# Token-major projections in chunks of 512 columns, with the first mixer's operand copied into class order

## The reference, cut to what matters

```python
# mixer of block 0 (A: banded attention, B: dilated attention)
qa, ka, va, qb, kb, vb = jnp.split(xn @ w_in, splits, axis=-1)   # va 256, vb 768 columns
# dilated attention gathers by stride: residue classes of the token number
t.reshape(bsz, sub, dil, B_SLOTS, dh).transpose(0, 2, 1, 3, 4)
# mixer of block 1
q, k, v = jnp.split(xn @ w_in, 3, axis=-1)                       # v 1024 columns
# mixer of block 2: of w_in_2, the columns i (512), vs (128), vw (128) and ng (24 gates)
...
```

## Time and profile before

| | us |
|---|---|
| median of 3 runs | 3481.54 |
| lowest and highest run | 3477.34, 3484.66 |
| span of the profiled execution, first to last instruction | 3476.3 |

### The profile page before, as it was taken

The page is one execution under the profiler, slowest core; times in us unless marked ns, Lnnn a source line. Parts: engine busy times, 40 slices in busy tenths (PEclk is TensorE's granted clock), DMA queues, the critical chain, the costliest instruction groups (busy, mean ns, idle before and its releaser), DMA issues.

```text
span 3476.3 us, 49224 instructions
## 1 busy us (share of the span) xinstructions
PE 3343.7 (96%) x16800; PEld 2705.7 (78%) x16800; DVE 1999.1 (58%) x2493; ACT 1753.2 (50%) x2114; POOL 1211.2 (35%) x625
## 2 busy tenths in 40 slices
PE   8999999999999999999999999899889999999996
PEld 6888888678888788888678888688766788787774
DVE  4335672663354433541463333457776699888888
ACT  5552212645533555321545533423563688888883
POOL 3444441044444444444134444342203222222224
PEclk9999999999999999999999999999999999999998
DMA  3225321023244222443422233222002899999997
GB/s 125 96 95 171 112 100 37 2 85 97 97 150 141 85 97 97 151 132 110 128 72 95 96 94 103 76 95 82 31 1 77 333 402 414 408 410 401 393 397 307
DMA packets 128103, 555.40 MB, mean 160 GB/s; under 512 B 19344, under 2 KB 19600, under 8 KB 100112
## 3 DMA queue, kind: packets, MB, share of 16 engines
q1 hardware_dynamic: 112896, 520.59, 41.5%
q0 software_dynamic: 14976, 33.58, 2.6%
q10 hardware_dynamic: 144, 0.08, 0.0%
HBM read 531.62 MB, written 41.94 MB: 165 GB/s over the span
## 4 chain that ended last, share of the span: by engine, by line
PE 60%; issue 25%; POOL 7%; DVE 5%; ACT 2%; DMA 1%; POOLq 0%; DVEq 0%; SPq 0%; ACTq 0%
PE ps L731 17%; PE ps L733 16%; PE ps L732 16%; POOL w_lo L1762 7%; PE ps L1189 2%; PE ps L751 1%; PE ps L892 1%; PE ps L1268 1%; PE ps L917 1%; PE ps L902 1%; PE ps L1018 1%; PE ps L1000 1%; PE ps L979 0%; DMA big<-in_exp_gu 0%; PE ps L1208 0%
## 5 line engine op out<-in xcount | busy, mean ns | idle before, releaser
L1762 POOL TENSOR_TENSOR w_lo<-stage_buf,w_hi 128x1024 fp32r<-128x1024 f32 (+1 forms) x396 | 971.8, 2454 | 1554.9 <-ACT w_hi L1344 1554.9
L1344 ACT ACTIVATE w_hi<-stage_buf 128x1024 fp32r<-128x1024 f32 (+1 forms) x396 | 413.9, 1045 | 1254.9 <-PE ps L733 1204.8
L731 PE MATMUL ps<-x_hi,w_hi 128*128 128x512 f32 x1984 | 776.1, 391 | 8.7 <-POOL w_lo L1762 7.9
L732 PE MATMUL ps<-x_lo,w_hi 128*128 128x512 f32 x1984 | 774.9, 391 | 0.0
L733 PE MATMUL ps<-x_hi,w_lo 128*128 128x512 f32 x1984 | 774.5, 390 | 0.0
L731 PE MATMUL ps<-hid,w_hi 128*128 128x512 f32 x1312 | 519.0, 396 | 2.6 <-issue 1.7
L733 PE MATMUL ps<-hid,w_lo 128*128 128x512 f32 x1312 | 511.7, 390 | 0.0
L732 PE MATMUL ps<-hid,w_hi 128*128 128x512 f32 x1312 | 510.8, 389 | 0.0
L731 PEld LDWEIGHTS ps<-x_hi,w_hi 128*128 128x128 f32 x1984 | 374.2, 189 | 90.7 <-POOL w_lo L1762 9.6
L733 PEld LDWEIGHTS ps<-x_hi,w_lo 128*128 128x128 f32 x1984 | 374.3, 189 | 78.0
L732 PEld LDWEIGHTS ps<-x_lo,w_hi 128*128 128x128 f32 x1984 | 374.2, 189 | 77.5
(11 more groups left out here) (388 smaller groups left out, 5121.8 us busy)
## 6 DMA issues: line engine op xcount, KB each, us to landing
stage_buf<-in_gu SPq DMA_DIRECT2D x176, 512.0 KB, 3.3
big<-in_exp_gu SPq DMA_DIRECT2D x72, 1024.0 KB
h_buf<-in_exp_gu SPq DMA_DIRECT2D x72, 1024.0 KB
s_buf<-in_exp_dn SPq DMA_DIRECT2D x72, 1024.0 KB
slot_rows<-stage_buf SPq DMA_DIRECT2D x72, 512.0 KB
stage_buf<-in_down SPq DMA_DIRECT2D x64, 512.0 KB, 3.6
stage_buf<-in_down SPq DMA_DIRECT2D x32, 384.0 KB, 3.1
sil_buf<-in_ada SPq DMA_DIRECT2D x24, 512.0 KB, 4.1
```

The lines of the kernel that those rows point to most:

```text
L731: nc.tensor.matmul(o, a_hi, b_hi, start=start, stop=False)
L732: nc.tensor.matmul(o, a_hi, b_lo, start=False, stop=False)
L1344: nc.scalar.activation(w_hi[s][:, 0:n], stage[s][:, 0:n], ACT.Copy).then_inc(upper_done, 1)
L1762: nc.gpsimd.tensor_tensor(w_lo[s][:, 0:n], stage[s][:, 0:n], w_hi[s][:, 0:n].bitcast(F32), ALU.subtract).then_inc(parted, 1)
```

## The change

A table gives each token-major phase its chunks: v_ab 256, 512, 256 columns; v_c 512, 512; tok_2 512, 280 (the columns of zeros are gone). A unit of a 512 or 280 column chunk holds 2 feature tiles in place of 4, so it has 24 matmuls; a unit of a 256 column chunk still has 48. Each phase still has 8 units, each transfer is still 512 KB, and ScalarE and GpSimd still split all 1024 floats of it. In mix_0, ScalarE writes a copy of `x_hi` and `x_lo` in class order into a part of `hid_buf` that is free then, one tile beside each of the first 16 units of in_ab, and chunks 1 and 2 of v_ab read the copy. VectorE evicts a whole chunk at once; in tok_2 the second chunk's values and gates are evicted together, after `first_norm`.

```diff
+V_WIDTHS = {"v_ab": [256, 512, 256], "v_c": [512, 512], "tok_2": [512, 280]}
...
+        _deep = 4 if _w == 256 else 2
+        CHUNKS[_name].append(dict(width=_w, deep=_deep, first=_at, units=KD // _deep, col=sum(_widths[:_c]),
+                                  by_class=_name == "v_ab" and _c > 0))
...
+        xc_hi, xc_lo = (tiles(hid_buf[:, a:a + KD * T], T) for a in (14336, 14336 + KD * T))
...
+            if beside:
+                with eng.Fori(0, beside) as i:
+                    turn(i, False)
+                work = None
+                for i in range(beside, turns):
+                    turn(i, False)
...
-                for c in range(units // 2):
-                    pe.wait_ge(evac_done, U + 2 * c)
+                for c, ch in enumerate(CHUNKS[phase]):
+                    width, deep, first = ch["width"], ch["deep"], ch["first"]
+                    hi, lo = (xc_hi, xc_lo) if ch["by_class"] else (x_hi, x_lo)
+                    pe.wait_ge(evac_done, U if c == 0 else U + 2 + CHUNKS[phase][c - 1]["first"])
...
+                    if c == 1 and ch["by_class"]:
+                        pe.wait_ge(x_classed, 2 * KD)
+                    for n in range(ch["units"]):
+                        s = (first + n) % 2
+                        pe.wait_ge(parted, CUT[phase] + first + n + 1)
...
+                            for kk in range(deep):
+                                k = deep * n + kk
+                                last = three(ps[:, 4 * ((c + 1) % 2) + t, 0:width], hi[:, k, tk], lo[:, k, tk],
...
+            def class_order(i, j):
+                if j == 0:
+                    act.wait_ge(units_done, u("in_ab"))
+                    act.wait_ge(x_ready, i + (PART_AT["mix_0"] + 1))
+                a, b = (x_hi_buf, 14336) if j == 0 else (x_lo_buf, 14336 + KD * T)
+                nc.scalar.activation(hid_buf[:, bass.ds(i * T + b, T)].rearrange("p (t i) -> p t i", t=4),
+                                     by_class(a[:, bass.ds(i * T, T)].bitcast(F32)), ACT.Copy).then_inc(x_classed, 1)
...
-                    weights("in_ab")
+                    weights("in_ab", class_order, beside=KD)
...
+                    if phase == "tok_2" and c == 1:
+                        nc.vector.tensor_copy(d, ps[:, b:b + 4, 0:pitch])
+                        ins = nc.vector.tensor_copy(gates, ps[:, b:b + 4, pitch:width])
...
-                    token_units("tok_2", 0, 2, R_VI, T)
+                    token_units("tok_2", 0, 1, R_VI, T)
                     first_norm()
-                    token_units("tok_2", 2, 1, R_VSW, 256)
+                    token_units("tok_2", 1, 1, R_VSW, 256)
                     hgrn_keys()
                     hgrn_first_levels()
-                    token_units("tok_2", 3, 1, R_GATE, 24, width=24)
                     hgrn()
```

More of the change, by code:

```diff
@@ L210, in block_kernel @@
         x_ready = sem("x_ready")
+        x_classed = sem("x_classed")
         sil_ready = sem("sil_ready")
@@ L480, in block_kernel, with each_unit @@
         ORDER = [ph for st in STAGES for ph in STAGE_PHASES[st]]
-        def each_unit(eng, phase, part, work=None, lead=None):
+        def each_unit(eng, phase, part, work=None, lead=None, beside=0):
             n = BASE[phase][1]
@@ L811, in token_major @@
             def token_major(phase):
[L813 to L818, removed]
-                for c in range(units // 2):
-                    pe.wait_ge(evac_done, U + 2 * c)
+                U = BASE[phase][0]
+                for c, ch in enumerate(CHUNKS[phase]):
+                    width, deep, first = ch["width"], ch["deep"], ch["first"]
+                    hi, lo = (xc_hi, xc_lo) if ch["by_class"] else (x_hi, x_lo)
+                    pe.wait_ge(evac_done, U if c == 0 else U + 2 + CHUNKS[phase][c - 1]["first"])
                     if c == 1 and phase == "tok_2":
@@ L1344, in upper, with weights @@
                 nc.scalar.activation(w_hi[s][:, 0:n], stage[s][:, 0:n], ACT.Copy).then_inc(upper_done, 1)
-            def weights(phase, work=None, lead=None):
-                each_unit(act, phase, upper, work, lead)
+            def weights(phase, work=None, lead=None, beside=0):
+                each_unit(act, phase, upper, work, lead, beside)
+            def class_order(i, j):
[5 more added lines that the diff above has]
+                                     by_class(a[:, bass.ds(i * T, T)].bitcast(F32)), ACT.Copy).then_inc(x_classed, 1)
             def squares(name, ready, n, ks=range(KD)):
@@ L2656, in _ @@
                     columns(st)
-                    token_units("v_ab", 0, 4, 20 * T, D)
+                    token_units("v_ab", 0, 3, 20 * T, D)
                     dve.sem_inc(FOLDED["ab"]["qkv"], 1)
@@ L2729, in _units, with _chunks @@
         n // width, P, (k // P) * width)
-def _halves(w):
-    n, _, cols = (u := _units(w, 256)).shape
-    return np.ascontiguousarray(u.reshape(n, P, 2, cols // 2).transpose(0, 2, 1, 3)).reshape(2 * n, P, cols // 2)
+def _chunks(phase, w):
+    out = np.zeros((8, P, UNIT), np.float32)
+    for ch in CHUNKS[phase]:
+        n, deep, width = ch["units"], ch["deep"], ch["width"]
+        part = w[:, ch["col"]:ch["col"] + width].reshape(n, deep, P, width).transpose(0, 2, 1, 3)
+        out[ch["first"]:ch["first"] + n, :, 0:deep * width] = part.reshape(n, P, deep * width)
+    return out
 def _column(v):
```

44 lines of the change are left out of this document (23 added, 21 removed).

## The result

The changed kernel takes 3440.5 us (median of four runs, 3437.4 to 3441.5) against 3481.6 us for the kernel before in the same sitting (four runs, 3477.3 to 3484.7): 41.1 us less, ratio 0.9885 with a 95% interval of 0.9871 to 0.9899. The forecast was 3441.6 us. The profiled execution took 3437.4 us with a span of 3435.6, where that of before has 3476.3: 40.7 us less.

The account below looks back on a forecast made before the run. TensorE, busy 96% of 3476.3 us, was taken as the bound, with VectorE's order deciding in the third mixer. Gains of 33.9 + 1.4 + 4.6 = 39.9 us took 3481.54 to 3441.6 us, range 3434 to 3450.

Parts of the forecast that it names:

- First mixer, 33.9 us: v_ab chunks 1 to 3: 67.2 us paced by slow class-order loads become 33.3 us with copy and wider chunks.
- The copies, 0: ScalarE's 16 class-order copies in in_ab, 0.7 to 1.2 us each, cost 0, covered by TensorE's and VectorE's work.
- Second mixer, 1.4 us: v_c: wide chunks save 2.6 us of matmuls, the longer bare last eviction takes back 1.1 us; net 1.4 us.
- Third mixer, 4.6 us: tok_2: TensorE done 14 us earlier, but VectorE's order lets only 4.6 us through, 3.9 of it before the keys.
- the bound of 2.5: Lower bound of the third mixer's gain, if a second norm multiply stands still and the clock falls.
- (a): First mixer: slow load comes from something that stays in v_ab; gain there 22.4 us, total 3453 us; chance 0.03.
- (b): Third mixer loses gain to a second split in the norm and the low clock: 3444 us; chance 0.2.
- (c): Third mixer gives all of TensorE's 14 us, VectorE's order mattering less: 3432 us; chance 0.03.
- (d): First mixer: the 16 strided copies hold up in_ab's weights; 6.9 us a copy would eat 39.9 us; chance 0.01.

## Why the prediction was right, point by point

**First mixer, 33.9 us.** Measured 33.90. Both steps are in the trace: the wide chunk at 5.44 us a unit took 21.79 (counted 21.8), the narrow one 11.51 (11.5). The cause was inferred from the code and from one pair of rows, 329 against 192 ns; the narrow chunks on the copied operand show it, with 189 ns. The prediction did not say how the gain divides. Copy first, the copy is worth 32.6 us and the width 1.3; width first, the width is worth 22.2 and the copy 11.7. They are two remedies for one thing.

**The copies, 0.** A copy took 1.11 us, inside 0.7 to 1.2 and at the strided end of it: 1.76 times the contiguous 0.63 us. It cost nothing, and three more beside each cost nothing.

**Second mixer, 1.4 us.** 1.45 us at attention's start, by the terms: 2.6 us of matmuls less, 1.1 us of bare eviction more. What the step left out is the clock behind the bare wait: in the profiled execution 0.7 us went back inside attention, and over the executions with this eviction the gain lies between 0.1 and 2.0. The term is right where it was taken and uncertain further on.

**Third mixer, 4.6 us.** Between the two profiles 5.06 us, the keys 4.2 us earlier (3.9 counted). The order of events was as written: TensorE idle for 9 us before its first product, the logarithm ahead of the norm's end, the norm stopped once, for 2.86 us, and VectorE without a gap from the norm to the keys. But the sum was made against an execution in which the clock had fallen after TensorE's wait of 2.09 us. That fall was read and priced at 1.7 us, and used only to ask whether a new wait might bring one; it was not asked whether the old one was part of the stage's 52.5 us. With the old chunks at full clock the stage takes 50.64 us, so against that the change is worth 3.2 us, and the term was 1.4 us too large. TensorE's lead was the other weak step: it was counted to be done 1.4 us before VectorE asks for the last chunk (2379.3 and 2380.7), and was 0.4 us ahead. A longer wait was feared only for the clock and GpSimd's split beside the norm; that a late weight unit could make VectorE wait for TensorE was not priced. In one of six executions it did, and the stage took 50.64 us with the new chunks: 1.9 us less than in the profile of before, below the bound of 2.5.

**The total.** 39.9 forecast, 41.1 between the medians and 40.7 between the spans. That close an agreement is partly luck, as the profiled executions show. The stage terms add up to 33.90 + 1.45 + 5.06 = 40.4, but at the first token copy of the expert stage (2644.39 before, 2607.17 after) the kernels stood 37.2 us apart: 0.6 us had been lost ahead of the first mixer (515.48 against 514.88), 0.7 went back in the second mixer's attention, and 1.8 more over stages whose code is the same. The last 3.5 us come from the expert stage, which no edit touches: from there to the end the changed kernel took 828.4 us, the kernel before 831.9, and the nine others with the same code there 831.1 to 834.9.

**The rivals.** (a) a slow load that stays in v_ab fell with the narrow chunks on the copy; wide chunks without it took 44.96 us, where this rival's price was 44.8. (b) did not come about in the changed kernel: the norm was stopped once, and the clock was 1.00 throughout tok_2. Half of it did in the kernel with narrow chunks, where a clock of 0.65 made the last unit 1.5 us longer; the norm was stopped once there too. (c) all 14 us of TensorE's time: its last matmul of tok_2 starts 13.3 us earlier in the stage (34.93 against 48.20), but the stage gave 3 to 5, and with it undone the median stood 37.6 us below the kernel before in its sitting in place of 41.1. (d) copies that hold up in_ab: even fourfold they did not.

## What to carry to other kernels

Compare the weight loads of one stage by the layout they read. Reading the stationary tile at a stride of four cost 32.6 of 67.2 us here, and the cure was a copy on an engine with idle time. When a saving on TensorE ends because another engine becomes the last, as in the third mixer, what remains is that engine's order: of the 13 us that TensorE saved there, 3 to 5 reached the end of the stage, and moving the norm or shortening a neighbour's instruction then gave 2 us each. How far ahead an engine is has to be read where its result is taken, not from its next long wait: 9 us of idle time stood beside a lead of 0.4 us. And before a stage's length in one profile is used as the base of a sum, look at the granted clock in it: the same code took 50.6 us at 1.00 and 52.5 at 0.95.

## What the hardware showed that was not expected

- VectorE's smallest instructions can be among its dear ones. One of 4 elements per partition took 2.39 us and one of 12 elements took 2.03 us, against 0.16 and 0.17 when no split of GpSimd ran; each ended within 0.02 us of the split. The first is not a cost of the change: in the kernel before the same stop fell on one of four multiplies of 128x512 behind it, which took 2.75 us where the others took 0.53. The Trainium skill ("SBUF — State Buffer", section "SBUF: two separate sides") says that one engine holds the port pair they share for a whole instruction while the other waits, and that VectorE asks for it with two inputs in SBUF or in a 2-port mode, which it names for `tensor_scalar`. The 4-element one and the norm's multiply have two inputs in SBUF. The 12-element one multiplies one tile by the constant -1, so only the 2-port mode would make it fit, and no run here shows in which mode it ran.
- A strided weight load is not slow by a fixed amount: 329 ns with 256 moving columns and 310 with 512, with the matmuls 233 and 236 ns apart, so it paces both widths alike.
- ScalarE at 91% busy in in_ab slowed neither TensorE (84.5 of 85 us busy, as with 37%) nor the transfers (DMA share 0.30 in both).
- Stretches at 1.2 GHz (a granted clock of 0.50, as from 2352 to 2356 us in the changed kernel) come and go between executions of the same code. The same scores of attention took 66.3 to 68.1 us with a mean granted clock of 0.95 or 0.90. The expert stage varied by 6.5 us over eleven executions of the same code. One profile can't tell 2 us in a kernel of this length unless both ends of the stretch are cut at its own events.
